# Passages between blocks with four quarter buffers, and stick-breaking queries padded to 128 rows

## What is computed

```python
for layer in range(DEPTH):                      # DEPTH = 2
    u = rmsnorm(h, mix_pre_g[layer])
    ...                                         # attention of the layer -> mixed
    h = h + rmsnorm(mixed, mix_post_g[layer])   # passage 0 (layer 0) and 2 (layer 1)
    u = rmsnorm(h, ffn_pre_g[layer])
    gu = u @ ffn_w_gate_up[layer]
    f = (silu(gu[..., :D_FF]) * gu[..., D_FF:]) @ ffn_w_down[layer]
    h = h + rmsnorm(f, ffn_post_g[layer])       # passage 1 (layer 0)

# stick-breaking attention, 16 heads of 64, causal and strict
z = einsum('bhqd,bhkd->bhqk', q, k) * scale
log_1m = where(strict, log_sigmoid(-z), 0.0)
acc = cumsum(log_1m, reverse=True) - log_1m
w = where(strict, exp(log_sigmoid(z) + acc), 0.0)
out = einsum('bhqk,bhkd->bhqd', w, v)
```

## Time and profile before

| | before |
|---|---|
| median of 3 runs | 1406.96 us (1406.94 to 1408.07) |
| the profiled execution | 1407.61 us, of which its span is 1405.6 us |
| TensorE busy | 1348.3 us (96% of the span) |
| DVE busy | 723.8 us (51%) |
| ACT busy | 539.3 us (38%) |
| POOL busy | 241.7 us (17%) |
| chain that ended last | TensorE 83%, DVE 8%, ACT 4%, POOL 3% |

### The profile page before, as it was taken

How to read it: one execution, slowest core, us unless ns; L and a number is a source line. 1 busy time by engine, 2 the same in 40 slices (tenths; PEclk the granted TensorE clock), 3 DMA queues, 4 the chain that set the end, 5 groups by cost and what they waited for, 6 DMA issues and landing times.

```text
span 1405.6 us, 17864 instructions
## 1 busy us (share of the span) xinstructions
PE 1348.3 (96%) x6687; PEld 1127.2 (80%) x6687; DVE 723.8 (51%) x997; ACT 539.3 (38%) x861; POOL 241.7 (17%) x181
## 2 busy tenths in 40 slices
PE   7888999999999999999998999999999999999997
PEld 5666888888788888888877888888887888888886
DVE  4777554537644454322466666665376444543223
ACT  5466565555323232222353443433553232223122
POOL 0333100022211111010111222222322111110002
PEclk9989999999999999999998999999999999999999
DMA  5311332132333332333221121120323333332331
GB/s 156 113 39 45 82 77 67 45 91 63 103 96 98 93 101 87 96 96 96 75 61 30 46 60 45 45 65 26 90 72 94 104 90 100 94 110 84 99 96 60
DMA packets 187219, 112.16 MB, mean 80 GB/s; under 512 B 8944, under 2 KB 181557, under 8 KB 187166
## 3 DMA queue, kind: packets, MB, share of 16 engines
q1 hardware_dynamic: 185356, 106.68, 26.0%
q0 software_dynamic: 640, 2.10, 0.6%
q10 hardware_dynamic: 1170, 2.66, 0.5%
HBM read 109.30 MB, written 4.74 MB: 81 GB/s over the span
## 4 chain that ended last, share of the span: by engine, by line
PE 83%; DVE 8%; ACT 4%; POOL 3%; issue 2%; DMA 0%; POOLq 0%; DVEq 0%; SPq 0%; ACTq 0%
PE banks L379 26%; PE banks L381 25%; PE banks L380 25%; PE banks L1558 3%; DVE w_lo L374 2%; ACT w_hi L367 1%; POOL residual L716 1%; PE banks L1366 1%; DVE u_lo L653 1%; DVE sq_sum L481 1%; DVE tf L643 1%; ACT u_hi L685 1%; PE banks L422 1%; ACT probsT_hi L1374 0%; PE banks L2080 0%
## 5 line engine op out<-in xcount | busy, mean ns | idle before, releaser
L379 PE MATMUL banks<-u_hi,w_hi 128*128 128x512 f32 (+1 forms) x1112 | 430.3, 387 | 17.2 <-DVE u_lo L653 10.1
L374 DVE TENSOR_TENSOR w_lo<-w_raw,w_hi 128x1024 fp32r<-128x1024 f32 (+2 forms) x200 | 292.8, 1468 | 277.4 <-ACT w_hi L367 277.4
L380 PE MATMUL banks<-u_lo,w_hi 128*128 128x512 f32 (+1 forms) x1112 | 422.5, 380 | 0.0
L381 PE MATMUL banks<-u_hi,w_lo 128*128 128x512 f32 (+1 forms) x1112 | 422.1, 380 | 0.0
L367 ACT ACTIVATE w_hi<-w_raw 128x1024 fp32r<-128x1024 f32 (+2 forms) x200 | 206.0, 1030 | 242.8 <-PE banks L381 242.8
L379 PEld LDWEIGHTS banks<-u_hi,w_hi 128*128 128x128 f32 x1112 | 213.6, 192 | 60.3 <-DVE u_lo L653 13.2
L381 PEld LDWEIGHTS banks<-u_hi,w_lo 128*128 128x128 f32 x1112 | 213.2, 192 | 39.0
L380 PEld LDWEIGHTS banks<-u_lo,w_hi 128*128 128x128 f32 x1112 | 213.5, 192 | 38.0 <-issue 1.0
L845 POOL TENSOR_TENSOR up<-up,gate 128x512 f32<-128x512 f32 x44 | 71.8, 1632 | 396.8 <-DVE up L869 355.8
L826 ACT ACTIVATE gate<-gate 128x512 f32<-128x512 f32 x44 | 27.8, 632 | 209.5 <-DVE gate L865 209.5
L1578 POOL TENSOR_TENSOR stick_lo<-stick,stick_hi 128x1280 fp32r<-128x1280 f32 x16 | 56.7, 3543 | 206.3 <-DVE stick_hi L1574 206.3
(11 more groups left out here) (236 smaller groups left out, 2035.2 us busy)
## 6 DMA issues: line engine op xcount, KB each, us to landing
w_raw<-in_ffn_w_gate_up_dram SPq DMA_DIRECT2D x88, 512.0 KB, 3.8
w_raw<-in_ffn_w_down_dram SPq DMA_DIRECT2D x30, 512.0 KB, 3.5
w_raw<-in_sb_w_qkv_dram SPq DMA_DIRECT2D x24, 512.0 KB, 3.8
w_raw<-in_ab_w_in_dram SPq DMA_DIRECT2D x17, 512.0 KB, 3.9
w_raw<-in_ffn_w_down_dram SPq DMA_DIRECT2D x16, 448.0 KB, 3.4
w_raw<-in_ab_w_out_dram SPq DMA_DIRECT2D x8, 512.0 KB, 3.6
w_raw<-in_sb_w_out_dram SPq DMA_DIRECT2D x8, 512.0 KB, 3.7
bias_by_distance<-bias_rows ACTq DMA_DIRECT2D x1, 2560.0 KB
```

The lines of the kernel that those rows point to most:

```text
L374: dve.tensor_tensor(wl[:, c.slot, 0:w], raw[:, c.slot, 0:w], wh[:, c.slot, 0:w].bitcast(F32), ALU.subtract).then_inc(w_lo, 1)
L379: nc.tensor.matmul(o, lh, rh, start=start, stop=False, skip_group_check=True)
L380: nc.tensor.matmul(o, lh, rl, start=False, stop=False, skip_group_check=True)
L381: return nc.tensor.matmul(o, ll, rh, start=False, stop=stop, skip_group_check=True)
```

## The change

**Passages.** `tf` becomes four buffers of 256 columns (`quarter`), used by both halves. `scaled` of slice n waits for the addition of slice n-4. DVE's list of a half starts with four `scaled`; chunk c's subtraction comes after them, then `lo(n)` and `scaled(n+4)` alternate, chunk c+1's subtraction stands after `scaled(6)`, that is, again ahead of `lo(3)`. ACT's list is reordered to match. The squares use the four buffers too.

**Small steps.** `stat_pe` of half 0 moves from behind the 4th to behind the 3rd slice (in `out_pe` and likewise in `dn_pe`), its `spread_pe` from behind 6 matmuls of the next chunk to ahead of them. In the gate-up the `spread_pe` moves from behind a tile's 24 matmuls into their middle.

**Stick-breaking.** Queries get a buffer of 128 rows per head, with zeros in the other head's 64 rows (written once, by four POOL memsets ahead of the block). `z_pe` contracts over all 128 rows, keys of both heads against the padded queries. Queries are rounded and subtracted in two instructions of 64 rows each.

```diff
@@ -255,3 +255,4 @@ def sb(stack, name, shape, dt=F32):
             sol = sb(s, "so_lo", [P, KD, T], F32R)
-            sq = [sb(s, f"sb_{n}", [P, 2, T], F32R) for n in ("q_hi", "q_lo", "k_hi", "k_lo")]
+            sq = [sb(s, f"sb_{n}", [P, 2, 2, T], F32R) for n in ("q_hi", "q_lo")] \
+                + [sb(s, f"sb_{n}", [P, 2, T], F32R) for n in ("k_hi", "k_lo")]
             lsp = sb(s, "softplus", [P, CW])
@@ -465,2 +467,6 @@ def add_squares(pool, n, k):
 
+        def quarter(n):
+
+            return tf[:, :, :].rearrange("p a n -> p (a n)")[:, (n % 4) * HALF:(n % 4 + 1) * HALF]
+
         def square_h(act, r, h, n, kh):
@@ -471,5 +477,6 @@ def square_h(act, r, h, n, kh):
             else:
-                if n > 2:
-                    act.wait_ge(hq_added, H_ADDS * r + (KD - 1) * h + n - 2)
-                dst = tf[:, n % 2, half(h)]
+                before = (KD - 1) * h + n - 4
+                if before > 0:
+                    act.wait_ge(hq_added, H_ADDS * r + before)
+                dst = quarter((KD - 1) * h + n)
             act.activation(dst, hT[:, n, half(h)], ACT.Square).then_inc(hq_ready, 1)
@@ -480,3 +487,3 @@ def add_h_squares(dve, r, h, n):
                 dve.wait_ge(hq_added, H_ADDS * r + (KD - 1) * h + n - 1)
-            nc.vector.tensor_tensor(acc[:, half(h)], acc[:, half(h)], tf[:, n % 2, half(h)], ALU.add)\
+            nc.vector.tensor_tensor(acc[:, half(h)], acc[:, half(h)], quarter((KD - 1) * h + n), ALU.add)\
                 .then_inc(hq_added, 1)
@@ -595,9 +602,6 @@ def out_pe(pe, ch, r, fn, k, o_at, o_rea
                     pe.wait_ge(f_read, F0[fn] + 4)
-                    half_products(HALF_BANK[n, 1], 1, c, range(4), 0, KD, o_at)
+                    half_products(HALF_BANK[n, 1], 1, c, range(3), 0, KD, o_at)
                     stat_pe(pe, k, R_BANK[r][0], (sq_added, AD0[k + 1]), 2 * r + 1, 0)
-                    half_products(HALF_BANK[n, 1], 1, c, range(4, KD), 0, KD, o_at).then_inc(w_used, 1)
-                elif n == NSPLIT_OUT + 1:
-                    half_products(HALF_BANK[n, 1], 1, c, range(2), 0, KD, o_at)
+                    half_products(HALF_BANK[n, 1], 1, c, range(3, KD), 0, KD, o_at).then_inc(w_used, 1)
                     spread_pe(pe, k, R_BANK[r][0], 0)
-                    half_products(HALF_BANK[n, 1], 1, c, range(2, KD), 0, KD, o_at).then_inc(w_used, 1)
                 else:
@@ -636,4 +640,4 @@ def scaled(h, n):
                 at = 2 * KD * r + KD * h
-                if n >= 2:
-                    dve.wait_ge(res_h, at + n - 1)
+                if KD * h + n >= 4:
+                    dve.wait_ge(res_h, at + n - 3)
                 if n == 0:
@@ -642,3 +646,3 @@ def scaled(h, n):
                     dve.wait_ge(f_read, F0[fn + 1] if h else F0[fn] + KD)
-                nc.vector.scalar_tensor_tensor(tf[:, n % 2, half(h)], F[:, n, half(h)],
+                nc.vector.scalar_tensor_tensor(quarter(n), F[:, n, half(h)],
                                                gains[:, g_post + n:g_post + n + 1], bank(R_BANK[r][h])[:, half(h)],
@@ -647,3 +651,3 @@ def scaled(h, n):
                     dve.wait_ge(res_t, at + 1)
-                    nc.vector.tensor_tensor(hT[:, 0, half(h)], hT[:, 0, half(h)], tf[:, 0, half(h)], ALU.add)\
+                    nc.vector.tensor_tensor(hT[:, 0, half(h)], hT[:, 0, half(h)], quarter(0), ALU.add)\
                         .then_inc(res_h, 1)
@@ -657,13 +661,15 @@ def lo(h, m):
             stat_dve(dve, k, None, None, 0)
-            split_lo(dve, Chunk(c))
             for h in range(2):
-                scaled(h, 0)
-                for n in range(1, KD):
+                for n in range(4):
                     scaled(h, n)
-                    lo(h, n - 1)
-                    if h == 0 and n == 3:
+                if h == 0:
+                    split_lo(dve, Chunk(c))
+                for n in range(KD):
+                    lo(h, n)
+                    if n + 4 < KD:
+                        scaled(h, n + 4)
+                    if h == 0 and n == 2:
                         split_lo(dve, Chunk(c + 1))
-                    if h == 0 and n == 5:
+                    if h == 0 and n == 4:
                         stat_dve(dve, k + 1, None, None, 1)
-                lo(h, KD - 1)
                 if h == 0:
@@ -688,22 +694,25 @@ def hi(h, n):
             hi(0, 0)
-            split_hi(act, Chunk(c + 1))
             hi(0, 1)
+            split_hi(act, Chunk(c + 1))
             hi(0, 2)
-            last_half(act)
             hi(0, 3)
+            last_half(act)
             hi(0, 4)
+            hi(0, 5)
             stat_act(act, k + 1, R_BANK[r][1], D, 1)
-            for n in range(5, KD):
-                hi(0, n)
             split_hi(act, Chunk(c + 2))
+            for n in range(6, KD):
+                hi(0, n)
             for n in range(KD):
                 hi(1, n)
-            for n in range(KD):
+            for n in range(4):
                 square_h(act, r, 0, n, k)
-                if n == 3:
-                    split_hi(act, Chunk(c + 3))
-            for n in range(KD):
+            split_hi(act, Chunk(c + 3))
+            for n in range(4, KD):
+                square_h(act, r, 0, n, k)
+            for n in range(4):
+                square_h(act, r, 1, n, k + 1)
+            split_hi(act, Chunk(c + 4))
+            for n in range(4, KD):
                 square_h(act, r, 1, n, k + 1)
-                if n == 2:
-                    split_hi(act, Chunk(c + 4))
             split_hi(act, Chunk(c + 5))
@@ -715,5 +724,5 @@ def res_pool(pool, r, last_add=None):
                     pool.wait_ge(res_t, 2 * KD * r + KD * h + n + 1)
-                    nc.gpsimd.tensor_tensor(hT[:, n, half(h)], hT[:, n, half(h)], tf[:, n % 2, half(h)], ALU.add)\
+                    nc.gpsimd.tensor_tensor(hT[:, n, half(h)], hT[:, n, half(h)], quarter(n), ALU.add)\
                         .then_inc(res_h, 1)
-                    if h == 0 and n == 1 and last_add:
+                    if h == 0 and n == 3 and last_add:
                         last_add(pool)
@@ -789,3 +798,3 @@ def tile(n0, i):
         def gu_pe(pe, ch, l, k):
-            def tile(n0, i, halves=(0, 1)):
+            def tile(n0, i, halves=(0, 1), inside=None):
                 c, b = gu_chunk(ch, n0, i), 2 * (n0 % 3)
@@ -797,3 +806,3 @@ def tile(n0, i, halves=(0, 1)):
                         pe.wait_ge(gu_read, base_wait(l, n0, i, half))
-                    project(pe, bank(b + half), cc, KD, P, 0, P, uh, ul).then_inc(w_used, 1)
+                    project(pe, bank(b + half), cc, KD, P, 0, P, uh, ul, inside=inside).then_inc(w_used, 1)
 
@@ -805,4 +814,3 @@ def base_wait(l, n0, i, half):
             stat_pe(pe, k, 6, (hq_added, H_ADDS * (2 * l + 1)))
-            tile(2, 0, (0,))
-            spread_pe(pe, k, 6)
+            tile(2, 0, (0,), lambda: spread_pe(pe, k, 6))
             tile(2, 0, (1,))
@@ -926,9 +934,8 @@ def hid(kk):
                 if j == 0:
-                    half_products(0, 1, c, range(4), k0, KF, hid)
+                    half_products(0, 1, c, range(3), k0, KF, hid)
                     stat_pe(pe, k, R_BANK[1][0], (sq_added, AD0[k + 1]), 3, 0)
-                    mm = half_products(0, 1, c, range(4, kt), k0, KF, hid)
+                    mm = half_products(0, 1, c, range(3, kt), k0, KF, hid)
                 elif j == 1:
-                    half_products(0, 1, c, range(2), k0, KF, hid)
                     spread_pe(pe, k, R_BANK[1][0], 0)
-                    mm = half_products(0, 1, c, range(2, kt), k0, KF, hid)
+                    mm = half_products(0, 1, c, range(kt), k0, KF, hid)
                 else:
@@ -1457,3 +1464,3 @@ def sb_item_act(act, p, par, j):
                 elif p == 0:
-                    act.wait_ge(v1_ready, 1)
+                    act.wait_ge(q_pad_ready, 1)
                 src = bank(P_BANK).rearrange("p (t h n) -> p t h n", t=TT, h=2)
@@ -1466,3 +1473,11 @@ def sb_item_act(act, p, par, j):
                 act.wait_ge(z_done, 2 * p - 2)
-            act.activation(sq[2 * j][:, par, :], tf[:, tf_sb(par, j), :], ACT.Copy).then_inc(qj_hi, 1)
+            if j == 0:
+                if isinstance(p, int) and p == 0:
+                    act.wait_ge(q_pad_ready, 5)
+                for e in range(2):
+                    r = slice(HD * e, HD * e + HD)
+                    ins = act.activation(sq[0][r, par, e, :], tf[r, tf_sb(par, j), :], ACT.Copy)
+                ins.then_inc(qj_hi, 1)
+                return
+            act.activation(sq[2][:, par, :], tf[:, tf_sb(par, j), :], ACT.Copy).then_inc(qj_hi, 1)
 
@@ -1481,4 +1496,11 @@ def sb_item_dve(dve, p, par, j):
                 dve.wait_ge(qj_hi, p * 3 + j + 1)
-                nc.vector.tensor_tensor(sq[2 * j + 1][:, par, :], tf[:, tf_sb(par, j), :],
-                                        sq[2 * j][:, par, :].bitcast(F32), ALU.subtract).then_inc(qj_lo, 1)
+                if j == 0:
+                    for e in range(2):
```

(19 more changed lines are left out.)

9 lines of the change are left out of this document (5 added, 4 removed).

## The result

| | before | changed |
|---|---|---|
| median, with the first profile | 1406.95 us (4 runs) | 1389.25 us (1386.93 to 1393.64, 4 runs) |
| ratio | | 0.9882, 95% interval 0.9864 to 0.9901 |
| the same kernel once more | 1407.44 us (11 runs) | 1391.41 us (1386.09 to 1395.34, 6 runs), ratio 0.9893 (0.9873 to 0.9913) |
| the profiled execution, its span | 1407.61, 1405.6 us | 1389.55, 1387.5 us |
| TensorE, DVE, ACT, POOL busy | 1348.3, 723.8, 539.3, 241.7 us | 1333.9, 730.9, 543.7, 252.6 us |

The change saves 16.6 us by the ratio. The measured time lies at the fast edge of my range (1389.5 to 1401.5): the median of 1389.25 is 0.25 us outside, the ratio gives 0.9882 x 1406.95 = 1390.4 and the second set 1391.41, both inside.

What follows compares the result with a forecast made beforehand. TensorE, busy 96% of the span, was taken as the bound. From 1407.6 us, 6.6 (passages), 2.5 (gate-ups) and 2.8 (`z_pe`) came off and 1.2 was added: 1396.9, forecast as 1396.3 since the median lies 0.65 lower; range 1389.5 to 1401.5.

Steps and rivals of the forecast that it cites:

- passages, at like clock: Three passages: 0.5 us from half 0 and 1.7 from half 1 in each, 6.6 us saved together.
- gate-ups: Both gate-ups: spread moved inside the tile removes TensorE's waits of 1.04 and 1.30 us; with restarts, 2.5 us saved.
- z_pe: Stick-breaking scores: padding to 128 rows saves 0.22 us per call (bounds 0.14 to 0.29), 2.8 us in 13 calls.
- start of stick-breaking: Block's start: splitting the queries' rounding and subtraction in two adds 0.60 us each on ACT and DVE, 1.2 us.
- Half 0, booked 0.5 us.: Passages, half 0: short waits at slices 1 and 2 go, the wait ahead of slice 3 stays at about 2 us.
- Half 1, booked 1.7.: Passages, half 1: four buffers bring a slice to 0.9 us instead of 1.22; TensorE's waits go, 1.7 us per passage.
- Squares. Nothing booked.: Passages, whole norm's sum: squares start some 2 us earlier, TensorE's `stat_pe` keeps its distance; if late, up to 1 us lost per passage.
- The clock, booked at nothing.: Passages, behind the wait at slice 3: clock falls as before, no gain; bounds nothing or the whole 3.2 us.
- 1 (whole durations, 1.22 us per slice): Half 1: DVE and POOL exclude each other for whole instructions, pace stays at 1.22 us; 1400.8 us, chance 0.14.
- 2 (padding worth nothing): Stick-breaking scores: the 0.1 us steps come from a change of operands, not rows; 1399.1 us, chance 0.12.
- 3: Passages: wait at slice 3 shortens enough for the clock to hold, 3.2 us each; 1393.1 to 1386.7 us, chance 0.16.
- 4: Stick-breaking turns: `nsp_lo` falls behind POOL's `stick_lo`, 2.6 us lost in each of seven turns; 1414 us, chance 0.03.

Runs made afterwards that it cites:

- again: The changed kernel once more, unaltered, for its scatter: 1391.41 us.
- c1_later: Changed kernel with chunk c+1's subtraction on DVE behind `u_lo` of slice 3 instead of ahead of it: 1381.32 us, 0.9834 against the kernel before.
- two_buffers: Changed kernel with two half buffers instead of four quarters, for scalings and squares, all orders kept: 1394.62 us, 0.9917 against the kernel before.
- buffers_only: Kernel before with four quarter buffers, for scalings and squares, in the old order: 1403.53 us, 0.9983 against the kernel before.
- one_input: Changed kernel with half 1's `u_lo` computed without subtracting `u_hi` (wrong output, for the pace alone): one execution, 1396.47 us, not to be compared.
- rows64: Changed kernel with 64-row queries and keys again, no padding, one rounding and one subtraction for the queries: 1393.59 us, 0.9914 against the kernel before.
- before_c1_later: Kernel before with one line moved, chunk c+1's subtraction behind `u_lo` of slice 3: 1402.29 us, 0.9977 against the kernel before.

## Why the prediction was right and where it fell short

The sign holds, and so do the mechanisms, but for the cause of half 1's pace, which I gave to the buffers and which was the order's. Term by term, forecast and what the traces show:

| term | forecast | shown |
|---|---|---|
| passages, at like clock | -6.6 | -7.8 |
| gate-ups | -2.5 | -2.7 |
| `z_pe` | -2.8 (13 calls) | -3.0 (last 12 calls; the first four are not told apart) |
| start of stick-breaking | +1.2 | +1.5 |
| sum | -10.7 | -12.0 |

The two estimates at like clock in `again`, 11.6 and 12.6 us, stand on either side of the 12.0; the rest of the 16 to 17 us is the clock's, an estimated 3 to 4.5.

- **Half 0, booked 0.5 us.** The size was wrong: slice 3 comes 3.78 us behind slice 0 instead of 3.82, so 0.04 us were gained up to there. "The long one stays at about 2 us" was right (1.92), and its cause, chunk c+1's subtraction, is shown by `c1_later`.
- **Half 1, booked 1.7.** The pace of 0.9 us was right (0.88), and so the waits went. Of the 2.8 us of passage 0 some 2.4 fall to it, when half 0 and the norm's sum (below) are taken off; the term was 0.7 too small. In the second profile of the kernel before, the two waits make 1.37 us of that; the rest are steps of 0.43 to 0.55 us between slices that now take 0.36, and I had booked too little for them. I put the gain down to four buffers; `two_buffers` and `buffers_only` show that the order did it. And the pace was right in part by luck: I had added 0.55 and 0.33, where `one_input` shows 0.77 for POOL by itself and 0.12 for `u_lo`.
- **"Squares. Nothing booked."** This step failed. Before, the eight matmuls of the norm's sum took 1.14 us to the next matmul (346.88 to 348.02), now 0.81 (339.38 to 340.19): 0.33 in each passage, 1.0 us in all. I had looked for a loss only. In `buffers_only` it is 0.81, in `two_buffers` 1.14: this part is the buffers'. Before, then changed:

```profile
346.88 1.05 PE L409 MATMUL banks<-ones,sq_sum 128*128 128x1 f32 x8
348.02 0.50 PE L379 MATMUL banks<-u_hi,w_hi 128*128 128x512 f32 x1
```

```profile
339.38 0.95 PE L411 MATMUL banks<-ones,sq_sum 128*128 128x1 f32 x8
340.19 0.48 PE L381 MATMUL banks<-u_hi,w_hi 128*128 128x512 f32 x1
```

- **`z_pe`.** 0.22 per call was low, 0.25 to 0.28 is right. I chose a middle value between one end gone and both, and both went.
- **The clock, booked at nothing.** This is the step that put the time at the edge of the range. The forecast took "the clock falls as before" as a fixed loss. It varies: 0.90 and 0.95 in the same passage of the same kernel before, 0.89 and 0.94 after. The runs of the changed kernel have a higher clock on average (0.9817 against 0.9787 in `again`), worth an estimated 3 to 4.5 us of the 16. Why isn't settled; `rows64`, with the same passages, averages 0.980 beside 0.9801 for before. What a longer stay costs depends on the kernel: before, 1.1 us in passage 0 (33.00 against 31.91), after, 1.6 in passage 1 (30.73 against 29.16).
- **A reading of the earlier trace rows.** "Passage 0 takes 27 us" took the length of the stretch asked for as that of the passage. The three passages take 33.00, 33.48 and 32.67 us, and the waits of their half 1 differ. No term of the sum used the 27.
- **Rivals.** 1 (whole durations, 1.22 us per slice) is refuted by the pace of 0.88. 2 (padding worth nothing) by the loop. 3 did not happen: the wait at slice 3 is as long as before. Its price was about right for the changed kernel (1.6 us between a long stay and a short one, 1.5 between a short one and none in `c1_later`) and too high for the kernel before (`before_c1_later`). 4 did not happen: in the turn near 895 us `nsp_lo` starts at 895.12 and `stick_lo` at 895.28, as far apart as in the earlier trace rows.

## What to carry to other kernels

Where two engines hand slices to each other, first look which instruction stands at the head of the list waiting for something just begun. Putting independent work ahead of it (four scalings, then subtraction and scaling in turn) bought the pace here with two buffers as with four. A subtraction of 1.3 us for data needed later, placed ahead of 0.4 us that TensorE waits for, cost the wait and the clock behind it. One moved line gained 7 to 8 us in the changed kernel and 3 in the one before: there TensorE spent the time won on waits in half 1. So ask which engine sets the pace of the stage behind before a gain is booked.
